# In the first layer's FFN the conditioning product of 44 weight tiles goes from TensorE to VectorE

## The reference, cut to what matters

```python
def adaln_params(cvec, w_ada, b_ada):
    m = jax.nn.silu(cvec) @ w_ada + b_ada          # [1024] @ [1024, 6144]
    return jnp.split(m, 6, axis=-1)                # shift, scale, gate; twice

def conv_ffn(h, w_up, conv_w, w_down):
    up = h @ w_up                                  # [512, 1024] @ [1024, 5632]
    a, b = up[..., :D_FF], up[..., D_FF:]
    return (jax.nn.silu(dwconv3(a, conv_w)) * b) @ w_down
```

## Time and profile before

| | |
|---|---|
| timed runs | 2238.44, 2242.71, 2242.76 us |
| the profiled execution, whole | 2227.43 us |
| its span, first to last instruction | 2225.6 us |
| TensorE matmul busy | 2133.4 us (96%) |
| VectorE busy | 1301.4 us (58%) |
| ScalarE busy | 1088.8 us (49%) |
| GpSimd busy | 478.8 us (22%) |
| mean granted TensorE clock | 0.98 of 2.4 GHz |
| first layer's FFN | about 276 to 680 us of the span |

### The profile page before, as it was taken

One profiled execution on the slowest core, in us unless ns is written; L12 is line 12 of the kernel. 1 busy time (PEld: TensorE's weight loads), 2 busy tenths in 40 slices (PEclk: granted clock), 3 DMA queues, 4 the chain that ended last, 5 costly groups with the idle time before them and its releaser, 6 DMA issues.

```text
span 2225.6 us, 44485 instructions
## 1 busy us (share of the span) xinstructions
PE 2133.4 (96%) x19108; PEld 2011.2 (90%) x19108; DVE 1301.4 (58%) x2526; ACT 1088.8 (49%) x1880; POOL 478.8 (22%) x226
## 2 busy tenths in 40 slices
PE   6999999999999989998899998999999999999998
PEld 4977999999998789998778888999999999999998
DVE  3445453343334666666663456498478897666665
ACT  4433352232235455445442545555567776655564
POOL 1201100000002120001110342088856663000000
PEclk9999999999998999999999999999999999999999
DMA  7235324444454346764233335465544445665563
GB/s 264 109 133 181 120 90 148 158 156 164 166 173 149 117 159 204 243 210 152 76 133 121 117 97 176 145 209 189 182 129 147 146 148 171 192 197 192 196 192 132
DMA packets 97284, 355.01 MB, mean 160 GB/s; under 512 B 10688, under 2 KB 11712, under 8 KB 96704
## 3 DMA queue, kind: packets, MB, share of 16 engines
q1 hardware_dynamic: 97088, 352.18, 47.4%
HBM read 351.09 MB, written 1.05 MB: 158 GB/s over the span
## 4 chain that ended last, share of the span: by engine, by line
PE 83%; DVE 5%; ACT 4%; DMA 3%; issue 2%; POOL 2%; SPq 0%; DVEq 0%; ACTq 0%; POOLq 0%
PE ps L79 78%; PE ps L84 4%; DVE TL L114 2%; ACT TH L158 2%; PE ps L107 1%; DMA RAW<-in_wdn 1%; POOL TL L114 1%; ACT SQ L155 1%; DMA RAW<-in_wada 1%; ACT Hh L158 1%; DMA RAW<-in_wup 1%; POOL SM L114 0%; DVE X L126 0%; DVE ps L114 0%; DMA RAW<-in_win 0%
## 5 line engine op out<-in xcount | busy, mean ns | idle before, releaser
L158 ACT ACTIVATE TH<-RAW 128x1024 fp32r<-128x1024 f32 (+1 forms) x515 | 540.3, 1050 | 408.5 <-PE ps L79 182.5
L114 DVE TENSOR_TENSOR TL<-RAW,TH 128x1024 fp32r<-128x1024 f32 (+1 forms) x343 | 421.3, 1228 | 450.2 <-ACT TH L158 449.9
L114 POOL TENSOR_TENSOR TL<-RAW,TH 128x1024 fp32r<-128x1024 f32 x172 | 414.0, 2410 | 513.0 <-ACT TH L158 486.8
L79 PE MATMUL ps<-Hh,TL 128*128 128x256 f32 x1920 | 450.7, 287 | 20.8 <-ACT Hh L158 9.6
L79 PE MATMUL ps<-Hh,TH 128*128 128x256 f32 x1920 | 438.7, 281 | 0.0
L79 PE MATMUL ps<-Hl,TH 128*128 128x256 f32 x1920 | 438.5, 281 | 0.0
L79 PE MATMUL ps<-HXh,TL 128*128 128x256 f32 x1312 | 367.9, 284 | 5.9 <-POOL TL L114 2.5
L79 PEld LDWEIGHTS ps<-Hh,TL 128*128 128x128 f32 x1920 | 320.9, 191 | 50.6 <-issue 21.3
L79 PE MATMUL ps<-HXh,TH 128*128 128x256 f32 x1312 | 362.2, 280 | 0.0
L79 PE MATMUL ps<-HXl,TH 128*128 128x256 f32 x1312 | 361.5, 280 | 0.0
L79 PE MATMUL ps<-W,TH 128*128 128x256 f32 x2048 | 348.2, 277 | 0.0
(11 more groups left out here) (323 smaller groups left out, 3004.3 us busy)
## 6 DMA issues: line engine op xcount, KB each, us to landing
RAW<-in_wada SPq DMA_DIRECT2D x144, 512.0 KB, 3.6
RAW<-in_ut SPq DMA_DIRECT2D x128, 512.0 KB, 3.5
RAW<-in_v SPq DMA_DIRECT2D x128, 512.0 KB, 4.3
RAW<-in_wup SPq DMA_DIRECT2D x88, 512.0 KB, 4.3
RAW<-in_win SPq DMA_DIRECT2D x74, 512.0 KB, 4.4
RAW<-in_wdn SPq DMA_DIRECT2D x32, 512.0 KB, 4.4
RAW<-in_wout SPq DMA_DIRECT2D x24, 512.0 KB, 3.7
RAW<-in_wq SPq DMA_DIRECT2D x16, 512.0 KB, 4.2
```

The source lines that it names most:

```text
L79: return self.e.matmul(out, lhs, rhs, start=first, stop=last, skip_group_check=skip)
L114: return DRY if self.e is None else self.e.tensor_tensor(out, a, b, op)
L158: return DRY if self.e is None else self.e.activation(out, a, ACT.Copy, **kw)
```

## The change

For the eleven groups 13 to 23 (`ADA_ADDED`, 44 tiles of the second layer's matrix) VectorE makes the products: for each half tile of 512 columns and each of the two vectors it multiplies by the column of `SC` and adds to a sum in SBUF (`ADA_SUM`, two buffers by group parity). A tile is four instructions of 128 x 512. TensorE runs eight matmuls per group over the sum, with a stationary operand of ones (`UNIT`). A conditioning tile of these groups now lets its `RAW` buffer go when VectorE's products of it are done (`ada_tile`). The table of points moves too: the attention units of layer 0 get 32 tiles instead of 24, the FFN of layer 0 44 instead of 52. With `m` from 1 on each `wup` pair has one tile behind it, and only block 16 has one between. The second silu of `c` is computed in the last attention unit, and the turn of group 9 goes from the output projection into the units.

```diff
-    plan += [(("unit", 0, u), 24 * (u + 1) // 16 - 24 * u // 16) for u in range(16)]
+    plan += [(("unit", 0, u), 2) for u in range(16)]
...
-            plan += [(("between", 0, m), 1)] * (m >= 12) + [(("up", 0, m), 1)] * (m > 1)
+            plan += [(("between", 0, m), 1)] * (m == 16) + [(("up", 0, m), 1)] * (m > 0)
...
+ADA_ADDED = range(13, 24)
...
+        def ada_sums(g):
+            pe.wait_ge(D, "ada_sum", g, 1)
+            pe.wait_ge(A, "arow", g - 1)
+            for st in range(2):
+                for z in range(4):
+                    last = pe.mm_at(ADA_BANK[32 * z:32 * z + 2, 0:128], UNIT[st], ADA_SUM[g % 2][st][:, 128 * z:128 * z + 128],
+                                    (0, 32 * z), st == 0, st == 1)
+            last.then_inc(*P.mark("ada_sums", g))
...
+        def ada_tile(b, i):
+            w, g = at_tile["wada", b, i], 12 * b + i // 4
+            if i % 4 == 0:
+                dve.wait_ge(A, "sc", b)
+            dve.wait_sem(f"ring_in{w % NRAW}", s_ring[w % NRAW], 16 * (w // NRAW + 1))
+            for kk in range(2):
+                src, c = raw(w)[:, 512 * kk:512 * kk + 512], 2 * (2 * (i % 4) + kk)
+                for st in range(2):
+                    o, by = ADA_SUM[g % 2][st][:, :], SC[:, c + st:c + st + 1]
+                    if i % 4 == 0 and kk == 0:
+                        last = dve.ts(o, src, by, None, ALU.mult)
+                    else:
+                        dve.wait_ge(D, "ada_sum", g, st)
+                        last = dve.stt(o, src, by, o, ALU.mult, ALU.add)
+                    last.then_inc(*D.mark("ada_sum", g, st))
+            D.note("ada_tile", w)
...
         def ada(*point):
             for b, i in ada_of(*point):
                 if point[0] != "gap" and 12 * b + i // 4 > 3:
                     lows(at_tile["wada", b, i] + AHEAD)
...
+                if g in ADA_ADDED:
+                    ada_tile(b, i)
+                    if i % 4 == 3:
+                        columns(g - 1)
...
             if i >= NRAW:
                 last = i - NRAW
-                if not order[last][3]:
+                if order[last][0][0] == "wada" and 12 * order[last][0][1] + order[last][0][2] // 4 in ADA_ADDED:
+                    sp.wait_ge(D, "ada_tile", last)
+                elif not order[last][3]:
                     sp.wait_ge(P, "used", last)
                 else:
                     sp.wait_ge(G if order[last][4] else D, "low", last)
```

More of the change, by code:

```diff
@@ L389 @@
 ADA_PLAN = _ada_plan()
-ADA_TURNED = (1, 3, 9, 35)
+ADA_TURNED = (1, 3, 35)
+ADA_ADDED = range(13, 24)
 ADA_PLACE = {1: 2, 2: 1}
@@ L400, in ada_place, with ada_steps @@
     return ADA_PLACE.get(g, g)
+def ada_steps(g, i):
+    return g - 1 if g - 1 in ADA_ADDED and i % 4 == 1 else None, g - 1 if i % 4 == 2 else None
 def ada_of(*point):
@@ L443, in emit @@
     FG, SC = SM[:, 0:8], SM[:, 8:24]
+    UNIT = [SM[:, 84:86], SM[:, 86:88]]
     nlam_lp, nlam_le, nlam, sg = ([SM[:, a + n * l:a + n * l + n] for l in range(DEPTH)]
@@ L472, in emit @@
         y.OC = [sb(f"l{l}oc{i}", 512, at=phase) for i in range(3)]
+        if l == 0:
+            ADA_SUM = [[sb(f"AS{i}{st}", 512, at=phase) for st in range(2)] for i in range(2)]
         phase.close()
@@ L640, in ada @@
                 w, g = at_tile["wada", b, i], 12 * b + i // 4
+                if g in ADA_ADDED:
+                    summed, turned = ada_steps(g, i)
+                    if summed:
+                        ada_sums(summed)
+                    if turned:
+                        columns(turned)
+                    continue
                 if i == 0:
@@ L914, in tensor_program @@
                          ks=MIX_ORDER, midway=lambda n: head_spread(1) if n == 4 else None)
-            if l == 0:
-                columns(9)
             for i in range(2, 8):
@@ L951, in tensor_program @@
                     ada("down", l, third, i)
+                    if (l, third, i) == (0, 2, 7):
+                        ada_sums(ADA_ADDED[-1])
         norm(("final",), 512)
@@ L1259, in highs, with ada_row @@
                 act.copy(high(i), raw(i)).then_inc(*A.mark("high", i))
+        def ada_row(g, *made):
+            act.wait_ge(P, *made)
+            if g > 1:
+                act.wait_ge(P, "adac", g - 2)
+            act.copy(AROW[g % 2][:, :], ADA_BANK[:, 0:128]).then_inc(*A.mark("arow", g))
+            if g in (11, 23):
+                act.act(SC, par("c1" if g == 11 else "c2"), ACT.Silu).then_inc(*A.mark("sc", g // 12 + 1))
         def ada(*point):
@@ L1265, in ada @@
                     highs(at_tile["wada", b, i] + AHEAD)
[L1266 to L1272, removed]
+                if g in ADA_ADDED:
+                    summed = ada_steps(g, i)[0]
+                    if summed:
+                        ada_row(summed, "ada_sums", summed)
+                elif i % 4 == 3:
+                    ada_row(g, *used("wada", b, i))
         def gap(*norm):
@@ L1530, in scalar_program @@
                     ada("down", l, third, i)
+                    if (l, third, i) == (0, 2, 7):
+                        ada_row(ADA_ADDED[-1], "ada_sums", ADA_ADDED[-1])
                     if third == 2:
@@ L1788, in ada @@
                     lows(at_tile["wada", b, i] + AHEAD)
-                g = 12 * b + i // 4 - 1
-                if i % 4 == 0 and g >= 0 and g not in ADA_TURNED:
-                    columns(g)
+                g = 12 * b + i // 4
+                if g in ADA_ADDED:
+                    ada_tile(b, i)
+                    if i % 4 == 3:
+                        columns(g - 1)
+                elif i % 4 == 0 and g and g - 1 not in ADA_TURNED:
+                    columns(g - 1)
         def gap(*norm):
@@ L1865, in vector_program @@
         dve.memset(ADA_BANK[:, :], 0.0).then_inc(*D.mark("ada_zero"))
+        dve.memset(SM[:, 84:88], 1.0).then_inc(*D.mark("unit0"))
+        dve.wait_ge(D, "unit0")
+        dve.memset(SM[:, 85:87], 0.0).then_inc(*D.mark("unit"))
         for l in range(DEPTH):
```

## The result

| | timed median (us) | lowest to highest | profiled span |
|---|---|---|---|
| before | 2241.39 (4 runs) | 2238.44 to 2242.76 | 2225.6 |
| after | 2419.87 (4 runs) | 2417.78 to 2423.27 | 2416.0 |

The ratio is 1.0794, 95% interval 1.0771 to 1.0816. The change makes the kernel 178.5 us slower. 2436 was forecast, with 2375 to 2490 as the range.

What follows compares the result with a forecast made beforehand. TensorE was taken as the bound before; after, a closed VectorE-to-transfer loop adds +188.5 us in the FFN and the units +4.4. With +193 on 2242.7 the forecast was 2436 us, range 2375 to 2490.

Steps and rivals of the forecast that it cites:

- The wait: First layer's FFN: VectorE frees the buffer its next `TL` needs, a closed loop through SyncE, transfer and ScalarE per tile.
- Up loop: One up-projection block of the FFN with its new tile: 15.24 us against 11.66 before, 19 of them 289.6 us.
- Down loop: One down-projection tile of the FFN with its new tile: 11.50 us against 6.21 before, 16 of them 184.0 us.
- The tile: Four products on VectorE per conditioning tile: 3.0 us, 2.46 for a group's first, mean 2.87.
- Last third: Six loops in the FFN's last third, with 384 KB tiles: 10.12 us each, 60.7 us in all.
- The odd ones: Two irregular intervals around block 16 of the FFN, put at 12.25 and 10.8 us.
- The start: Attention units before the FFN: eight more tiles cost +4.4 us; the FFN's first new tile was put at 305.1.
- The clock: TensorE's granted clock may fall in the loops' waits of 4 to 6 us; nothing was put on it.
- TensorE's share: TensorE's busy part of the FFN: about 70% in up blocks and 50% in down tiles.
- Rival 1: VectorE takes the FFN work in and TensorE stays the bound: 2224.5 us, chance 0.06.
- Rival 2: Low clock makes TensorE the bound of up blocks: 132 us more, 2568, chance 0.04; another 0.06 for part or slower transfers.
- rival 3: The FFN loop exists but is shorter, by products at 0.48 or down landings at 4.5: 2300 to 2385 us, chance 0.12.

Runs made afterwards that it cites:

- t3: The changed kernel with each conditioning tile's products made one point earlier on VectorE, same work on every engine; 2227.23 us, ratio 0.9961.
- t6: The changed kernel, products in place, but the first layer's FFN splits run one tile ahead instead of two; 2240.19 us, ratio 0.9998.
- t3b: Second run of the changed kernel with each tile's products one point earlier; 2220.97 us, ratio 0.9954.
- t1: The changed kernel's table of points alone, all conditioning tiles' products on TensorE as before the change; 2247.08 us, ratio 1.0018.
- t4: The changed kernel with its 154 multiply-and-add instructions cut from 512 to 8 columns; 2329.21 us, ratio 1.0405.
- t5: The table of points of the kernel before, groups 13 to 23 on VectorE, products one point earlier; 2223.72 us, ratio 0.9945.
- t7: Old table and products one point earlier, with groups 11 and 12 on VectorE too, all 52 FFN tiles; 2215.00 us, ratio 0.9924.

## Why the prediction was right

By the marks the change costs +177.6 us where the working had +193. (The two profiled executions lie 190.4 us apart, nearly the forecast; that is luck, since 13.3 of it is the pace of the last stage, described below.) The mechanism was the one forecast, and the sizes go as follows.

- **The wait.** Right. "VectorE sits idle through the transfer, ScalarE's copy": the chain shows just that, and t3 and t6 took it away by opening the loop alone.
- **Up loop**, forecast 15.24: 19 of them take 282.6 us, a mean of 14.87, so -7.0. Without the tile the chain's turn is 12.24, against 12.37.
- **Down loop**, forecast 11.50: 16 take 168.9 us, mean 10.56, so -15.1. This is the term most off. The landing was taken at 5.1 from the median of before; the chain of the kernel after has 4.37 to 4.75 for `wdn`, near the lower bound of 4.51. That is about 0.5 of the 0.94 us a turn, and the shorter tile 0.27. The lower bound was in the earlier trace rows, and the median was chosen over it. Why the landings are shorter here was not tested; in the down tile above a transfer lands at 446.07 and the next is issued only at 451.8.
- **The tile**, forecast 2.87: 2.73, or 2.20 for the first of a group, mean 2.60. It is 0.27 of the misses of both loops. A product's record is about 0.75 us long, as taken, but four of them take 2.73 and not 3.0, since each starts before the record of the one in front has ended. The upper bound of 1.0 us is nearly reached only beside GpSimd, at 0.94.
- **Last third**, forecast 6 x 10.12 = 60.7: 62.5, +1.8. The tiles are longer there (below). The odd ones 21.1 against 23.05; the tail 6.56 against 6.7.
- **The start.** The first new tile ends at 319.81, not 305.1. This is the step that failed: the units were priced at +4.4 us, eight tiles, and cost +15.0. I took the splits there as ready when TensorE comes. With this table GpSimd's are not: 4.7 us in three waits, and 1.2 in two for VectorE's, the same in all six profiles of this table. What differs between the six is the granted clock. The attention matmuls of the units, from the first to the last start, before, then t3b, then after:

```profile
L107 PE MATMUL ps<-P,l0att x48: 272/273/331, 104.9 to 212.1; 128*128 128x128 f32 x48
L107 PE MATMUL ps<-P,l0att x48: 272/273/445, 105.7 to 223.0; 128*128 128x128 f32 x48
L107 PE MATMUL ps<-P,l0att x48: 272/273/407, 106.3 to 228.2; 128*128 128x128 f32 x48
```

  They take 107.2, 117.3 and 121.9 us. In t3b the clock stays at 1.00 from 96 to 216 us, and the 10.1 us more are about what the eight tiles and the waits come to (4.4 + 5.9). In t3 it is 0.99 and they take 118.7, in t1, t4 and t6 0.97 and 120.2 to 120.4, in the kernel after 0.96 and 121.9. So up to 4.6 us go with the lower clock. That is an ordering of six profiles, and no run set the clock.

```profile
96.00:216.00 120.00, 113.54 (x1173) 90.45 (x1171) 59.24 (x151) 43.90 (x109) 7.44 (x3) 1.00 0.43 149
```

- **Behind the FFN** -3.4 us to the second mark, where nothing was forecast; less than the 6 us that two profiles of one kernel differ by, and not explained.

These sum to +15.0 + 166.0 - 3.4 = 177.6. The two misses partly cancel: 22.5 us too much in the FFN and 10.6 too little in the units.

- **The clock.** Nothing was put on it. In the FFN that was right, in the units not (above). In the FFN it was granted at 0.94 in the up blocks and 0.84 in the down tiles. A down tile has TensorE busy 60.70 / 8 = 7.6 us instead of 5.8 (5.66, and 0.14 for a quarter of a group's sum), but in a turn of 10.4; the longer matmuls lie inside its waits. (The working has 2 x 5.55 for a down tile at half the clock; by the row it is 2 x 5.66 = 11.3, still under its 11.5.)
- **TensorE's share**: forecast 70% and 50%, it was 82% (73.33 of 89.57) and 73% (60.70 of 83.22). Work at full clock would be 75% and 56% of these turns (11.11 + 0.14 of 14.9, 5.66 + 0.14 of 10.4); the rest goes with the slower clock, whose longer matmuls count as busy. The forecast's shares are about those of its own, longer loops (73% and 49%), with no clock in them.
- **The rivals.** Rival 1 fell with the 43 waits of TensorE for `TL`. Its 2224.5 us is what the same work takes once the order is different (t3, t3b). Rival 2 isn't there: no up block takes 22 us. Of rival 3 a part holds: the shorter landings are worth 16 x 0.5 = 8 us of the 10 in its text, the shorter products of the 35 full-size loops 35 x 0.27 = 9 of its 41.

## What to carry to other kernels

Free time on an engine is not room. Before work moves to an idle in-order engine, ask which buffer it holds, who waits for that buffer, and whether that tile comes back to the same engine as its next instruction; if so, the whole round of transfer and copy is paid each time, here 178 us for 18 of relief. The cure was not less work, but the same work one turn earlier in the queue. The Trainium skill, "Perfetto Trace Analysis" (section "Optimization Strategy"), reads a gap that repeats as a sign that buffers may be short; here there are 43 gaps of TensorE with a ring of four. But t3 and t6 closed them with the same four buffers, and no run had a fifth, so whether a fifth would have helped stays open.

## What was not expected of the hardware

**Products beside GpSimd.** In the last third four products take 3.75 us instead of 2.73. The rows of GpSimd and VectorE in the kernel after:

```profile
831.74 3.75 DVE L126 SCALAR_TENSOR_TENSOR AS<-RAW,SM,AS 128x512 f32<-128x512 f32 x4
832.63 1.65 POOL L114 TENSOR_TENSOR ACC<-ACC,SQ 128x512 f32<-128x512 f32 x1 [8.44 <-ACT SQ L155]
```

GpSimd's addition starts inside the four, and they take 1.02 us more; where it is not there, they take 2.73 again. The same stands in t5 and t7 (3.77 beside 1.66). The Trainium skill, "Advanced Engine Details and Errata" (section "GPSIMD Details"), says that GpSimd shares a read and a write interface with VectorE and that instructions with two inputs from SBUF conflict; the trace agrees. No run took GpSimd's addition away.

**Instructions that overlap.** A product is 745 ns in the records, and it is 0.66 us from the start of one to the start of the next. The Trainium skill, "Perfetto Trace Analysis" (section "Optimizing Scalar/DVE Operations"), says that part of a profiled latency overlaps with the next instruction; the trace agrees, with about 0.08 us of overlap.

**Two paces of TensorE.** The last stage takes 347.5 us in some profiles (before, t4, t3b, t5) and 360.8 in the others (after, t1, t3, t6, t7). Before, then t1, each at full granted clock and TensorE without a gap:

```profile
1900.00:1950.00 50.00, 50.00 (x443) 50.00 (x442) 31.32 (x37) 29.99 (x38) 0.00 (x0) 1.00 0.62 192
```

```profile
1900.00:1950.00 50.00, 50.00 (x427) 50.00 (x426) 31.31 (x36) 28.17 (x36) 0.00 (x0) 1.00 0.60 189
```

443 matmuls in 50 us against 427, 113 and 117 ns each. The same kernel (t3, t3b) shows both. The timed runs of before spread over 27 us (2224.28 to 2251.60) beside t1, and over 24 us beside t5. A pace that differs by 13 us can be half of that; what sets it, and what the rest of the spread is, stays open. Versions that differ by 10 us can only be compared over many timed runs.
